# Sums of a Strassen-like product turned into additions, partly made by accumulating DMA transfers, and splits moved between turns

## The chip, the cores and the metric

The kernel runs on one core of one Trainium2 chip. The time is the device time of one execution in microseconds (us). Five engines run side by side with their own instruction streams and meet through semaphores: TensorE (matmuls, named PE in the rows, its weight loads PEld), VectorE (DVE), ScalarE (ACT), GpSimd (POOL) and SyncE (SP). SP, ScalarE and GpSimd also issue DMA transfers (SPq, ACTq, POOLq); 16 DMA engines carry them out.

## The reference

One encoder layer for x of 1024 rows by 2048 columns, all float32:

```
h      = rmsnorm(x) * norm_w
proj   = h @ w_in                     # 2048 -> 4*1024 (attention) + 2*512 + 3*1024 (mLSTM) + 16 gates
attn   = dilated window attention, 8 heads of 128, 3 patterns mixed, q and k normed and rotated
attn  *= silu(z_a)
hm     = mLSTM forward + mLSTM backward, 4 heads (qk 128, v 256), rmsnorm per head
hm     = sigmoid(o_m) * hm * silu(z_m)
x_out  = x + concat(attn, hm) @ w_out # 2048 -> 2048
```

## The kernel before, in words

**Products.** Both projections are one list of 80 groups (GROUPS, line 48). A group makes two output tiles of 128 columns for all 1024 rows, with half of the inner dimension (kh 0 or 1, that is 1024 of 2048). From the third group on it does so by Winograd's form of Strassen's scheme: seven products of a 128x512 weight sum and a 512x512 sum of x's (or y's) blocks, in place of eight. Each float32 operand is split into a rounded part (hi) and the rest (lo), so a product is 12 matmuls of 512 columns: hi*hi, hi*lo, lo*hi for four pieces of 128 (lines 816 to 820). One product is a turn, u, from 14 to 559; g, n = divmod(u, 7). All engines walk the same list of turns in program order, and each has in every turn its share written out: that order and the semaphores are the whole schedule.

**A turn on VectorE** (from line 1895): softmax steps of an attention head; the eviction of product u-1 out of PSUM into xt, for n = 1, 3, 4, 5, 6 (evict, line 1343; ScalarE evicts n = 0 and 2); w_lo of turn u+2 (weight_lo, line 1337); gates; split work; mLSTM or attention steps; sums of y; and one of four weight sums (s_one to s_four) for n = 2, 3, 4, 6. Products alternate between two PSUM banks, so TensorE's turn u+1 waits for the eviction of product u-1. ScalarE makes w_hi of turn u+2 in turn u, after product u-1.

**x's and y's operands.** STAGE (line 54) names the groups at which the right operands are exchanged: group 16 (second half of x, b = 1), 48 (first half again, b = 2), 64 (first half of y, the mLSTM's, b = 3), 72 (second half, the attention's, b = 4). BUILD_AT (line 64) is the turn at which the last group before it starts: 105, 329, 441, 497; an offset counts from there. Operand n may be overwritten once product n of that last group is done, and is read at offset 7 + n. The seven operands are four blocks of x (n = 0, 2, 5's and 6's sources) and the sums T1 to T4 (n = 4, 1, 3, 5), each 512x512, on the chip as 128 partitions by 2048. ScalarE rounds one (t_high, 1083), VectorE takes the rest (t_low, 1442): one such pair is a split. For b = 2 the four sums' splits (KEPT = 1, 3, 4, 5) are loaded from t_dram, where b = 0 left them (t_loads, 514). For b = 3, 4 the operand comes from DRAM into t_lo, ScalarE rounds it into t_hi (y_operands, 1239), VectorE subtracts (y_low, 1829); Y_SPLIT (66) gives the offset of each.

**y's sums** (SUMS = 3, 1, 5, 4, in ty_dram). For the mLSTM's half SP loads three blocks of y of 1 MB at turn 321 (YM_AT) into the arena, VectorE makes three sums over whole blocks, SP stores them; a fourth follows from turn 339 on (ym_loads 657, ym_sums 1801). For the attention's half ya_sums (1816) runs in each head's offset 22: heads 0 to 3 one sum of the head's two halves, stored by SP at 23; heads 4 to 7 three sums with what head h-4 left, which SP loads at 21 and, but for head 7, stores at 23.

**Attention.** Head h starts at turn 357 + 17 h (A_START), so offset 22 of one head is offset 5 of the next. At 4 and 5 VectorE rotates 32 rows of q and of k (rotate, 1698); GpSimd stores them to rot_dram and loads them back in another order (turned_rows, 1953); SP loads the norms, broadcast to all partitions, at 5 and 6 (line 626); VectorE's norm of q and k at 8 and 9 (normed, 1716) reads both and TensorE's scores from 10 on (988) wait for it. SP loads v at 8, z at 9 over ystage, the head's output of before.

**Queues.** SP's queue carries the weights (next_weights, 460), stores of xt, the rows for each mLSTM step (549), loads for heads, and t_dram. GpSimd's carries accumulating stores of xt (added, 1931) and the rotary rows. mLSTM head j starts at turn 112 + 49 j; its y is stored at its offset 61 (m_out). Groups 41 to 47 have no accumulating store.

## Time and profile before

| | us |
|---|---|
| median of 3 runs | 1996.13 (1993.84 to 2001.1) |
| the profiled execution | 1991.36 |
| its span, first to last instruction | 1989.6 |
| TensorE busy | 1947.4 |
| VectorE busy | 1384.3 |
| ScalarE busy | 889.3 |
| GpSimd busy | 222.0 |

The page is one execution. A matmul's end is modelled, and successive matmuls overlap in it, so TensorE's turns are best measured from start to start of their first matmul. The rows of a timeline give start, duration, engine, line, and in brackets the idle time before it and what ended it. The windows give the busy time of each engine in a stretch, the granted clock of TensorE (1.00 is full), the share of the DMA engines' time and what they moved. Groups by form give the count, the busy time and the mean of one.

### The profile page before, as it was taken

To read this page: it belongs to the slowest core of one execution; us is meant where nothing else is said; L and a number is where in the kernel's file an instruction comes from. 1 tells how busy PE (TensorE), PEld (TensorE's weight loads), DVE (VectorE), ACT (ScalarE), POOL (GpSimd) and SP (SyncE) were. 2 spreads that over 40 slices of the span, in tenths; PEclk is the share of its full clock that TensorE was granted. 3 is DMA by queue.
4 is the path that set the end of the run, shared out by engine and by line. 5 is a ranking of instruction groups with operands and counts; after the bars stand their busy time and mean duration, and the time that the engine had idled before them with its cause. 6 is when DMAs were issued, how large, how long until landed. Compare 5 with 4: busy or idle time off the path is not lost.

```text
span 1989.6 us, 27114 instructions
## 1 busy us (share of the span) xinstructions
PE 1947.4 (98%) x9089; PEld 1589.4 (80%) x9089; DVE 1384.3 (70%) x2791; ACT 889.3 (45%) x1422; POOL 222.0 (11%) x240
## 2 busy tenths in 40 slices
PE   8999999999999999999999999999999899999999
PEld 6888887888888888888887878787787677777787
DVE  7677868678768768767767575665666857667655
ACT  6554335344335435334453335545446463455222
POOL 0241000110110010010000111110110111111111
PEclk9999999999999999999999999999999899999999
DMA  6676543564564465365369864462655836347554
GB/s 210 218 272 229 190 160 113 139 151 126 134 162 119 108 159 148 107 159 148 115 206 369 208 154 92 116 175 50 169 121 131 263 75 191 99 119 209 104 117 106
DMA packets 159337, 310.37 MB, mean 156 GB/s; under 512 B 17072, under 2 KB 36048, under 8 KB 155488
## 3 DMA queue, kind: packets, MB, share of 16 engines
q1 hardware_dynamic: 128432, 247.81, 37.8%
q0 software_dynamic: 28608, 53.49, 17.3%
q10 hardware_dynamic: 2160, 7.34, 1.0%
q8 instruction: 74, 1.21, 0.3%
q14 instruction: 63, 0.52, 0.1%
HBM read 198.60 MB, written 118.37 MB: 159 GB/s over the span
## 4 chain that ended last, share of the span: by engine, by line
PE 84%; DMA 5%; DVE 5%; issue 4%; ACT 1%; SPq 0%; POOL 0%; DVEq 0%; ACTq 0%; POOLq 0%
PE ps L816 22%; PE ps L820 21%; PE ps L818 21%; PE ps L1019 3%; PE ps L988 2%; PE ps L1005 2%; DMA arena<-rot_dram 1%; PE ps L957 1%; PE ps L913 1%; PE ps L922 1%; PE ps L916 1%; PE ps L1023 1%; DMA rot_dram<-arena 1%; ACT w_hi L1056 1%; PE ps L1021 1%
## 5 line engine op out<-in xcount | busy, mean ns | idle before, releaser
L816 PE MATMUL ps<-t_hi,w_hi 128*128 128x512 f32 x2184 | 872.0, 399 | 24.4 <-issue 9.7
L820 PE MATMUL ps<-t_hi,w_lo 128*128 128x512 f32 x2184 | 853.5, 391 | 0.0
L818 PE MATMUL ps<-t_lo,w_hi 128*128 128x512 f32 x2184 | 853.2, 391 | 0.0
L816 PEld LDWEIGHTS ps<-t_hi,w_hi 128*128 128x128 f32 x2184 | 411.5, 188 | 125.3 <-issue 45.9
L820 PEld LDWEIGHTS ps<-t_hi,w_lo 128*128 128x128 f32 x2184 | 411.2, 188 | 87.7
L818 PEld LDWEIGHTS ps<-t_lo,w_hi 128*128 128x128 f32 x2184 | 412.1, 189 | 79.6
L1340 DVE TENSOR_TENSOR w_lo<-s_tmp,w_hi 128x512 fp32r<-128x512 f32 x312 | 221.5, 710 | 180.0 <-ACT w_hi L1056 169.2
L1056 ACT CAST w_hi<-s_tmp 128x512 fp32r<-128x512 f32 x312 | 193.9, 622 | 292.7 <-PE ps L820 273.2
L1340 DVE TENSOR_TENSOR w_lo<-w_raw,w_hi 128x512 fp32r<-128x512 f32 x234 | 165.4, 707 | 146.9 <-ACT w_hi L1056 140.6
L1056 ACT CAST w_hi<-w_raw 128x512 fp32r<-128x512 f32 x234 | 145.4, 621 | 225.4 <-PE ps L820 225.3
L413 POOL DMA_DIRECT2D fin_dram<-xt x32 | 28.1, 878 | 850.8 <-ACT xt L1069 829.7
L1064 ACT COPY xt<-ps 128x512 f32<-128x512 f32 x78 | 45.8, 587 | 110.5 <-PE ps L820 110.4
L1200 ACT ACTIVATE arena<-arena,sums 128x704 f32<-128x704 f32 x64 | 56.4, 882 | 79.0 <-DVE sums L1744 79.0
L1069 ACT COPY xt<-ps 128x512 f32<-128x512 f32 x78 | 45.6, 585 | 98.6 <-PE ps L820 98.3
L1370 DVE TENSOR_TENSOR xt<-ps,xt 128x512 f32<-128x512 f32 x78 | 53.8, 689 | 47.4 <-PE ps L820 46.7
L1156 ACT ACTIVATE arena<-arena,g_cols 128x128 f32<-128x128 f32 x64 | 25.9, 405 | 132.1 <-DVE arena L1601 132.1
L1194 ACT ACTIVATE arena<-arena,mins 128x704 f32<-128x704 f32 x64 | 56.7, 887 | 49.1 <-DVE mins L1738 49.0
L1354 DVE TENSOR_TENSOR xt<-ps,xt 128x512 f32<-128x512 f32 x78 | 53.6, 688 | 26.2 <-PE ps L820 25.6
L1373 DVE TENSOR_TENSOR xt<-ps,xt 128x512 f32<-128x512 f32 x78 | 53.7, 688 | 23.6 <-PE ps L820 23.5
L988 PE MATMUL ps<-arena 128*128 128x512 f32 x128 | 65.9, 596 | 3.4 <-DVE arena L1721 2.2
L1364 DVE TENSOR_TENSOR xt<-ps,xt 128x512 f32<-128x512 f32 x78 | 53.6, 688 | 17.2 <-PE ps L820 16.6
L1750 DVE COPY arena<-ps 128x256 f32<-128x256 f32 x64 | 27.0, 422 | 51.9 <-PE ps L1023 33.1
(225 smaller groups left out, 2390.5 us busy)
## 6 DMA issues: line engine op xcount, KB each, us to landing
w_raw<-w_all_dram SPq DMA_DIRECT2D x320, 256.0 KB, 4.0
fin_dram<-xt SPq DMA_DIRECT2D x128, 256.0 KB, 4.3
fin_dram<-xt POOLq DMA_DIRECT2D x128, 256.0 KB, 5.0
arena<-fin_dram SPq DMA_DIRECT2D x64, 512.0 KB, 7.3
outT_dram<-xt POOLq DMA_DIRECT2D x60, 256.0 KB, 4.1
arena<-xT_dram SPq DMA_DIRECT2D x44, 256.0 KB, 6.0
arena<-xT_dram SPq DMA_DIRECT2D x16, 512.0 KB, 4.4
outT_dram<-xT_dram SPq DMA_DIRECT2D x16, 512.0 KB, 5.4
```

The costliest lines, as they stand in the source:

```text
L816: nc.tensor.matmul(ps[:, bank, :], hi, t_hi[:, n, k, :], start=new and k == 0, stop=False, skip_group_check=True)
L818: nc.tensor.matmul(ps[:, bank, :], hi, t_lo[:, n, k, :], start=False, stop=False, skip_group_check=True)
L820: mm = nc.tensor.matmul(ps[:, bank, :], lo, t_hi[:, n, k, :], start=False, stop=k == KP - 1, skip_group_check=True)
L988: nc.tensor.matmul(ps[:, 4, :], q, by_class(a_k)[:, :, h * P:(h + 1) * P], start=True, stop=True)
L1019: nc.tensor.matmul(out, vtok[:, 4 * h + b, :], pT[:, b, :], start=b == 0, stop=False)
L1056: nc.scalar.copy(w_hi[:, b % 3, :], src).then_inc(hi_done, 1)
L1194: nc.scalar.activation(prob[:, i % 2, 0:KEYS], prob[:, i % 2, 0:KEYS], ACT.Exp, bias=mins[:, i % 2:i % 2 + 1], scale=-1.0, accum_out=sums[ ...
L1200: nc.scalar.activation(prob[:, i % 2, 0:KEYS], prob[:, i % 2, 0:KEYS], ACT.Copy, scale=sums[:, 2 + i % 2:3 + i % 2]).then_inc(a_p, 1)
L1340: nc.vector.tensor_tensor(w_lo[:, b % 3, :], src, w_hi[:, b % 3, :].bitcast(F32), ALU.subtract).then_inc(lo_done, 1)
L1354: nc.vector.tensor_tensor(x2, bank, x1, ALU.add).then_inc(ev_d, 1)
L1370: nc.vector.tensor_tensor(x1, bank, x1, ALU.add).then_inc(ev_d, 1)
L1373: nc.vector.tensor_tensor(x2, bank, x2, ALU.add).then_inc(ev_d, 1)
```

## The change

- Signs: T1 to T4, three evictions' results and the weight sums s_one and s_four are negated where needed, so that all sums over blocks of x and y are additions. Evictions n = 1 and 3 become -(bank) - x1 by scalar_tensor_tensor.
- y's sums of the mLSTM half: from turn 226 SP copies blocks of y within DRAM into ty_dram, and GpSimd adds other blocks to them by accumulating transfers, in six steps (YM_STEPS) that wait for one another. ym_loads, ym_sums and their arena tiles go, and so do waits of SP for them.
- y's sums of the attention half: heads 0 to 3 store their upper half for T3 and their one sum three times, at offset 22; heads 4 to 6 have no sum on VectorE, GpSimd adds the halves to three and then one of the sums in DRAM; head 7 adds on VectorE as before.
- Splits: one table of offsets for ScalarE and one for VectorE, for b = 1, 2 and for b = 3, 4. T4's four sums move from offsets 4 and 5 to 6, 7, 8, 9.

```diff
-Y_SPLIT = {3: {3: 0, 5: 1, 6: 2, 8: 3, 9: 4, 10: 5, 11: 6}, 4: {3: 0, 5: 1, 6: 2, 7: 3, 8: 4, 9: 5, 10: 6}}
+HIGH_AT = {1: {1: 0, 2: 1, 4: 2, 6: 3, 7: 4, 9: 6, 10: 5}, 2: {1: 0, 4: 2, 8: 6}}
+LOW_AT = {1: {1: 0, 3: 1, 5: 2, 7: 3, 8: 4, 10: 6, 11: 5}, 2: {1: 0, 5: 2, 8: 6}}
+Y_HIGH = {3: {3: 0, 4: 1, 5: 2, 7: 3, 8: 4, 9: 5, 10: 6}, 4: {3: 0, 5: 1, 6: 2, 7: 3, 8: 4, 9: 5, 10: 6}}
+Y_LOW = {3: {3: 0, 5: 1, 6: 2, 8: 3, 9: 4, 10: 5, 11: 6}, 4: {3: 0, 5: 1, 6: 2, 7: 3, 8: 4, 9: 5, 10: 6}}
 FILL_AT = 45
-YM_AT = 321
...
+YM_STEPS = (226, 231, 236, 322, 328, 333)
...
                 eng.wait_ge(m_out, 16 * M_HEADS)
-                eng.wait_ge(ym_out, 16 * len(SUMS))
+                eng.wait_ge(ym_added, 64)
             else:
-                eng.wait_ge(ya_out if n in SUMS else a_out, 16 * (KP if n in (0, 4) else ATT_HEADS - 1))
+                heads = KP if n in (0, 4) else ATT_HEADS - 1
+                if n == 4:
+                    eng.wait_ge(ya_out, 32 * KP)
+                elif n in SUMS:
+                    eng.wait_ge(ya_added, 32 * (heads - KP))
+                else:
+                    eng.wait_ge(a_out, 16 * heads)
...
                         sp.wait_ge(a_pv, 4 * h)
-                        sp.wait_ge(ya_out, 16 * h)
+                        sp.wait_ge(ya_out, 32 * min(h, KP))
...
                     if h > 0:
                         sp.wait_ge(a_out, 16 * h)
-                        sp.wait_ge(ya_out, 16 * h)
+                        sp.wait_ge(ya_out, 32 * min(h, KP))
+                    if h > KP:
+                        sp.wait_ge(ya_added, 32 * (h - KP))
...
-                if at == 21 and h >= KP:
+                if at == 21 and h == ATT_HEADS - 1:
                     sp.wait_ge(a_pv, 4 * h + 4)
-                    sp.wait_ge(a_out, 16 * (h - KP + 1))
-                    sp.wait_ge(ya_out, 16 * (h - KP + 1))
-                    sp.dma_start(y_sums[:, 0, :], y_dram[ATT_HEADS + h - KP][:, HALF:]).then_inc(ya_in, 16)
-                    sp.dma_start(y_sums[:, 1, :], ty_dram[1, SUMS.index(4)][:, h - KP, :]).then_inc(ya_in, 16)
+                    sp.wait_ge(ya_out, 32 * KP)
+                    sp.dma_start(y_sums[:, 0:2, :], ty_dram[1, 0:2, :, KP - 1, :].rearrange("i p s -> p i s")
+                                 ).then_inc(ya_in, 16)
                 if at == 22 and h < ATT_HEADS - 1:
                     sp.wait_ge(a_y, 4 * h + 4)
                     sp.dma_start(y_dram[ATT_HEADS + h], ystage).then_inc(a_out, 16)
-                if at == 23 and h < ATT_HEADS - 1:
-                    sp.wait_ge(ya_sum, sums_of_y(h + 1))
-                    if h < KP:
-                        sp.dma_start(ty_dram[1, SUMS.index(4)][:, h, :], y_sums[:, 0, :]).then_inc(ya_out, 16)
-                    else:
-                        sp.dma_start(ty_dram[1, 0:3, :, h - KP, :].rearrange("i p s -> p i s"), y_sums
-                                     ).then_inc(ya_out, 16)
-
-            def ym_loads(off):
+                if at == 22 and h < KP:
+                    sp.dma_start(ty_dram[1, SUMS.index(3), :, h, :], ystage[:, HALF:]).then_inc(ya_out, 16)
+                    sp.wait_ge(ya_sum, h + 1)
+                    sp.dma_start(ty_dram[1, 1:4, :, h, :].rearrange("i p s -> p i s"),
+                                 y_sums[:, 0, :].unsqueeze(1).to_broadcast([P, 3, HALF])).then_inc(ya_out, 16)
+
+            def ym_copies(u):
                 y = y_dram[0:ATT_HEADS].rearrange("k p s -> p k s")
-                if off == 0:
-                    sp.wait_ge(m_out, 16 * M_HEADS)
-                    sp.wait_ge(m_g, 2 * M_HEADS)
-                    sp.wait_ge(m_rms, M_HEADS)
-                    sp.wait_ge(m_upd, 16 * M_HEADS)
-                    sp.wait_ge(m_c, 16 * M_HEADS)
-                    sp.wait_ge(m_ops, 16 * M_HEADS)
-                    sp.dma_start(ym_a, y[:, 0:KP, 0:HALF]).then_inc(ym_in, 16)
-                    sp.dma_start(ym_b, y[:, 0:KP, HALF:]).then_inc(ym_in, 16)
-                    sp.dma_start(ym_c, y[:, KP:, HALF:]).then_inc(ym_in, 16)
-                if off in (5, 6, 7):
-                    n, at = ((4, ym_a), (3, ym_b), (1, ym_c))[off - 5]
-                    sp.wait_ge(ym_sum, off - 4)
-                    sp.dma_start(ty_dram[0, SUMS.index(n)], at).then_inc(ym_out, 16)
-                if off == 18:
-                    sp.wait_ge(ym_out, 48)
-                    sp.dma_start(ym_b, y[:, KP:, 0:HALF]).then_inc(ym_in, 16)
-                if off == 22:
-                    sp.wait_ge(ym_sum, 4)
-                    sp.dma_start(ty_dram[0, SUMS.index(5)], ym_b).then_inc(ym_out, 16)
+                if u == YM_STEPS[0]:
+                    sp.wait_ge(m_out, 16 * 2)
+                    for n in (4, 3):
+                        sp.dma_start(ty_dram[0, SUMS.index(n)], y[:, 0:KP, HALF:]).then_inc(ym_out, 16)
+                if u == YM_STEPS[2]:
+                    sp.wait_ge(ym_added, 16)
+                    sp.dma_start(ty_dram[0, SUMS.index(1)], ty_dram[0, SUMS.index(4)]).then_inc(ym_out, 16)
+                if u == YM_STEPS[4]:
+                    sp.wait_ge(ym_added, 48)
+                    sp.dma_start(ty_dram[0, SUMS.index(5)], ty_dram[0, SUMS.index(1)]).then_inc(ym_out, 16)
...
-                    nc.vector.tensor_tensor(x2, bank, x1, ALU.add).then_inc(ev_d, 1)
+                    nc.vector.scalar_tensor_tensor(x2, bank, -1.0, x1, ALU.mult, ALU.subtract).then_inc(ev_d, 1)
...
-                if off in (4, 5):
-                    t_four(1, 2 * off - 8)
-                    t_four(1, 2 * off - 7)
+                if off in (6, 7, 8, 9):
+                    t_four(1, off - 6)
...
             def ya_sums(h):
                 low, high = ystage[:, 0:HALF], ystage[:, HALF:]
+                if KP <= h < ATT_HEADS - 1:
+                    return
                 dve.wait_ge(a_y, 4 * h + 4)
                 if h < KP:
                     dve.wait_ge(a_pv, 4 * h + 4)
-                    nc.vector.tensor_tensor(y_sums[:, 0, :], high, low, ALU.subtract).then_inc(ya_sum, 1)
+                    nc.vector.tensor_tensor(y_sums[:, 0, :], high, low, ALU.add).then_inc(ya_sum, 1)
                     return
-                dve.wait_ge(ya_in, 32 * (h - KP + 1))
-                nc.vector.tensor_tensor(y_sums[:, 1, :], high, y_sums[:, 1, :], ALU.subtract).then_inc(ya_sum, 1)
-                nc.vector.tensor_tensor(y_sums[:, 0, :], high, y_sums[:, 0, :], ALU.subtract).then_inc(ya_sum, 1)
+                dve.wait_ge(ya_in, 16)
+                nc.vector.tensor_tensor(y_sums[:, 1, :], high, y_sums[:, 1, :], ALU.add).then_inc(ya_sum, 1)
+                nc.vector.tensor_tensor(y_sums[:, 0, :], high, y_sums[:, 0, :], ALU.add).then_inc(ya_sum, 1)
                 dve.wait_ge(ya_sum, sums_of_y(h) + 1)
-                nc.vector.tensor_tensor(y_sums[:, 2, :], low, y_sums[:, 1, :], ALU.subtract).then_inc(ya_sum, 1)
+                nc.vector.tensor_tensor(y_sums[:, 2, :], low, y_sums[:, 1, :], ALU.add).then_inc(ya_sum, 1)
 
             def y_low(b, off):
-                n = Y_SPLIT[b].get(off)
...
+            def add_ym(u):
+                y = y_dram[0:ATT_HEADS].rearrange("k p s -> p k s")
+                if u == YM_STEPS[1]:
+                    pool.wait_ge(m_out, 16 * 2)
+                    pool.wait_ge(ym_out, 32)
+                    pool.dma_start(ty_dram[0, SUMS.index(4)], y[:, 0:KP, 0:HALF], accum_op=ALU.add).then_inc(ym_added, 16)
+                if u == YM_STEPS[3]:
+                    pool.wait_ge(m_out, 16 * M_HEADS)
+                    pool.wait_ge(ym_out, 48)
+                    for n in (1, 3):
+                        pool.dma_start(ty_dram[0, SUMS.index(n)], y[:, KP:, HALF:], accum_op=ALU.add).then_inc(ym_added, 16)
+                if u == YM_STEPS[5]:
+                    pool.wait_ge(ym_out, 64)
+                    pool.dma_start(ty_dram[0, SUMS.index(5)], y[:, KP:, 0:HALF], accum_op=ALU.add).then_inc(ym_added, 16)
+
+            def add_ya(h, at):
+                if KP <= h < ATT_HEADS - 1:
+                    if at == 22:
+                        pool.wait_ge(a_y, 4 * h + 4)
+                        pool.wait_ge(ya_out, 32 * KP)
+                        pool.dma_start(ty_dram[1, 0:3, :, h - KP, :].rearrange("i p s -> p i s"),
+                                       ystage[:, HALF:].unsqueeze(1).to_broadcast([P, 3, HALF]), accum_op=ALU.add
+                                       ).then_inc(ya_added, 16)
+                    if at == 24:
+                        pool.wait_ge(ya_added, 32 * (h - KP) + 16)
+                        pool.dma_start(ty_dram[1, SUMS.index(5), :, h - KP, :], ystage[:, 0:HALF], accum_op=ALU.add
+                                       ).then_inc(ya_added, 16)
```

## Rows read from the trace of the kernel before

**Rows 1.** page, part 1 (busy us of each engine) and part 4 (chain of waits by engine).

```profile
PE 1947.4 (98%) x9089; PEld 1589.4 (80%) x9089; DVE 1384.3 (70%) x2791; ACT 889.3 (45%) x1422; POOL 222.0 (11%) x240
...
PE 84%; DMA 5%; DVE 5%; issue 4%; ACT 1%; SPq 0%; POOL 0%; DVEq 0%; ACTq 0%; POOLq 0%
```

**Rows 2.** TensorE timeline (start, duration): turns 106, 119, 326, 329, 343, 357, 425, 442, 459.

```profile
323.86 0.39 PE L816 MATMUL ps<-t_hi,w_hi 128*128 128x512 f32 x1
...
366.31 0.39 PE L816 MATMUL ps<-t_hi,w_hi 128*128 128x512 f32 x1
...
1047.39 0.39 PE L816 MATMUL ps<-t_hi,w_hi 128*128 128x512 f32 x1
...
1058.46 0.47 PE L816 MATMUL ps<-t_hi,w_hi 128*128 128x512 f32 x1 [0.42 <-DVE xt L1370]
...
1100.16 0.39 PE L816 MATMUL ps<-t_hi,w_hi 128*128 128x512 f32 x1
...
1138.24 0.39 PE L816 MATMUL ps<-t_hi,w_hi 128*128 128x512 f32 x1
...
1451.46 0.50 PE L816 MATMUL ps<-t_hi,w_hi 128*128 128x512 f32 x1
...
1531.79 0.50 PE L816 MATMUL ps<-t_hi,w_hi 128*128 128x512 f32 x1
...
1624.78 0.50 PE L816 MATMUL ps<-t_hi,w_hi 128*128 128x512 f32 x1
```

**Rows 3.** windows in head 5: span, busy of PE, PEld, DVE, ACT, POOL, clock, DMA, GB/s.

```profile
1565.00:1567.50 2.50, 0.00 (x0) 0.00 (x0) 2.46 (x4) 0.52 (x1) 1.22 (x3) 0.94 1.06 294
1567.50:1570.00 2.50, 0.55 (x1) 0.50 (x2) 2.50 (x5) 1.22 (x2) 0.87 (x1) 0.50 1.06 403
1570.00:1572.50 2.50, 2.50 (x7) 1.98 (x6) 1.80 (x2) 1.21 (x1) 0.75 (x2) 0.50 1.09 298
```

**Rows 4.** groups by form on VectorE: count, busy us, mean ns, idle before.

```profile
L1354 DVE TENSOR_TENSOR xt<-ps,xt 128x512 f32<-128x512 f32 x78 | 53.6, 688 | 26.2 <-PE ps L820 25.6
...
L1450 DVE TENSOR_TENSOR t_lo<-arena,t_hi 128x2048 fp32r<-128x2048 f32 x14 | 32.1, 2290 | 5.6 <-ACT t_hi L1104 5.5
...
L1861 DVE SCALAR_TENSOR_TENSOR arena<-arena,ncol 128x512 f32<-128x512 f32 x12 | 8.2, 749 | 0.0
...
L1807 DVE TENSOR_TENSOR arena<-arena 128x2048 f32<-128x2048 f32 x1 | 2.3, 2285 | 0.0
```

**Rows 5.** DMA: queues (packets, MB, share of 16 engines), then issues (KB, us to landing).

```profile
q1 hardware_dynamic: 128432, 247.81, 37.8%
q0 software_dynamic: 28608, 53.49, 17.3%
...
outT_dram<-xT_dram SPq DMA_DIRECT2D x16, 512.0 KB, 5.4
...
t_lo<-t_dram SPq DMA_DIRECT2D x4, 1024.0 KB, 9.8
```

**Rows 6.** windows while the kept splits are loaded, columns as before; first and last of six.

```profile
1065.00:1070.00 5.00, 4.41 (x20) 3.38 (x19) 4.26 (x6) 2.92 (x3) 0.00 (x0) 1.00 1.00 363
...
1090.00:1095.00 5.00, 4.00 (x18) 3.02 (x18) 3.47 (x6) 1.24 (x2) 0.37 (x1) 1.00 1.03 345
```

**Rows 7.** timeline of SP's queue, VectorE, GpSimd in heads 1, 5 and 6: start, duration.

```profile
1235.35 0.38 SPq L626 DMA_DIRECT2D arena<-rs_dram  x1
...
1239.77 0.32 SPq L652 DMA_DIRECT2D ty_dram<-arena  x1
...
1246.79 2.05 DVE L1721 SCALAR_TENSOR_TENSOR arena<-arena,spare 128x1024 f32<-128x1024 f32 x1
...
1562.30 0.68 DVE L1824 TENSOR_TENSOR arena<-arena 128x512 f32<-128x512 f32 x1
...
1562.90 0.69 DVE L1825 TENSOR_TENSOR arena<-arena 128x512 f32<-128x512 f32 x1
...
1663.23 0.55 POOL L1962 DMA_DIRECT2D arena<-rot_dram  x1 [4.23 <-DMA rot_dram<-arena]
```

54 lines of the change are left out of this document (20 added, 34 removed).

## The prediction, made before the changed kernel was run

> **What bounds the kernel now.** I read the page's engine totals first: TensorE is busy 98% of 1989.6 us, VectorE 70%, and 84% of the chain of waits is TensorE [rows 1]. So a cheaper VectorE pays only where TensorE stands still or is late. Next I took TensorE's own rows and asked how long one weight product (a turn: 12 matmuls) lasts. Undisturbed, 14 turns take 1138.24 - 1100.16 = 38.08 us, 2.72 us a turn [rows 2]. Stretches against that pace:
> - the splits of x's second half (turns 106 to 118): 366.31 - 323.86 = 42.45 us for 13 turns, 35.4 at the pace: 7.1 us late;
> - the four sums of the mLSTM's y (turns 326 to 328): 1058.46 - 1047.39 = 11.07 us for 3 turns: 2.9 late;
> - the splits of x's first half (329 to 342): 1100.16 - 1058.46 = 41.7 us for 14: 3.6 late;
> - head 5 of the attention, beside which y's first splits lie: 1624.78 - 1531.79 = 92.99 us, and head 4 before it 80.33 us: 12.7 late [rows 2].
> All else that the change touches lies where TensorE keeps its pace, apart from about 1 us a head while the rotary rows come. What fills the four stretches is VectorE: a split costs it 2.29 us, a sum over one of y's blocks 2.29, a sum over one head's half 0.69, or 0.61 where they follow each other [rows 4, 7]. It must take a product out of PSUM (0.69) before TensorE may use that bank again two turns later.
> The granted clock is the second cost. While TensorE stood still in head 5 (0.00 us busy of 2.5), it went from 1.00 over 0.94 to 0.50, that is from 2.4 to 1.2 GHz, and stayed there for 5 us [rows 3]; exposed, that loses 2.5 us.
>
> **The change part by part**, on the profiled execution's own time, 1991.36 us (1.8 of it outside the span). It stands 4.8 us under the median of the runs, 1996.13; differences are added to the median.
>
> *Splits of x's second half: -0.5.* The sums T4 (4 of 0.61) and seven splits (2.2 from start to start) are all still there, 17.8 us, but end at offset 11 instead of 9. I walked VectorE turn by turn: an eviction 0.61, w_lo 0.61, an s sum 0.61. Before, offsets 4 and 5 hold two T4 sums and a split each (5.3 and 4.6 us in a turn of 2.72), so TensorE waits for evictions. After, no turn has over 4.0 (offset 7: eviction, w_lo, one T4, one split). VectorE falls behind by about 1 us in each of offsets 7, 8, 10 and 11. The waits come at product 3 of group 16 (1.2 us) and at product 5, whose split is made one turn before it is read (3.3 us). Its end comes out 1.7 us earlier than now. But the 3.3 us wait stands at the end of the stretch, where VectorE no longer hides a lower clock; at the 5 us of half clock of [rows 3] that gives back up to 2.5. Bounds -1.7 and +0.8; I take the middle.
>
> *y's sums of the mLSTM half leave VectorE: -2.9.* Three of the four whole-block sums (2.29 each, [rows 4]) lie in turns 326 to 328 and are the only extra work there; without them evictions are on time, so the 2.9 goes. The fourth (turn 342) costs TensorE nothing now.
>
> *What replaces them.* Per 1 MB the hardware queue's packets take 37.8% x 1989.6 / 247.8 = 3.0 us of all 16 DMA engines, the software queue's, nearly all of them accumulating, 17.3% x 1989.6 / 53.5 = 6.4 us [rows 5]. The change has four copies of 1 MB within DRAM and four accumulations of 1 MB, for 8 MB of loads and stores: 38 us of DMA for 24. A copy within DRAM of 512 KB lands in 5.4 us now [rows 5]. At turns 226 to 236 TensorE keeps its pace, and each new wait has some 5 turns (14 us) for one transfer. Behind the two copies in SP's queue stand k and q of mLSTM head 2, read four turns on; behind SP's wait at turn 236 the rows of an mLSTM step, behind that at turn 328 the weights of group 48, read four turns on; behind GpSimd's only its stores. I take +0.3 (0 to 3). At turns 322 to 333 VectorE's stores go, but the last accumulation (6.4 us of DMA) becomes ready just when eight 1 MB loads of kept splits run. There the DMA engines are full (1.00 and 1.03 at 363 and 345 GB/s, first and last of six such windows [rows 6]), and the t_lo load takes 9.8 us in the median [rows 5]. Wholly in their way it makes products 339 to 341 6.4 us late, with nothing to hide it; ready before them, 0. I take +2.0. The split of block 2 is made by VectorE a turn after ScalarE's half instead of waiting for it: -0.6 of the 3.6, or nothing.
> Here the Trainium skill, "DMA: Bandwidth & Descriptors", section "Issuing engines are not separate DMA queues", speaks against the change: transfers of all issuing engines end on the same 16 DMA engines and interleave, so moving work to GpSimd's queue makes no bandwidth. By that rule the whole 6.4 counts and the sum is 4.4 us higher; the windows at 1.00 say the engines are full, not whose transfer waits.
>
> *Head 4's three sums (3 x 0.61) leave VectorE, and ScalarE's y splits go a turn earlier: -2.5.* They lie in the very turn that makes product 449 late: the first start at 1562.30 and 1562.90 [rows 7]. Walked again, the eviction comes 1.8 us earlier, and the half that ScalarE makes earlier saves VectorE waits of 0.7. The half clock still costs what VectorE waits for TensorE, 1.1. Bounds -1.0 (more DMA at the same place: 0.75 MB accumulating is 4.8 us) and -5.0 (clock stays up).
>
> *Heads 0 to 3: +1.0.* SP now waits for VectorE's sum one turn earlier, before it loads the first broadcast row: in head 1 that load is issued at 1235.35, the store behind the sum at 1239.77 [rows 7]. So it comes 4.9 us later, behind 0.75 MB of stores (2.3 us). Landing some 7.7 us after issue (a median 5.4 to 5.7 for such a size, and the stores), it comes at 1247.9, and its reader starts at 1246.79 now [rows 7]: so about 1 us of that shows on VectorE. But the second norm, which TensorE waits for, hangs on GpSimd's rotary rows. And v's load at offset 8, with z behind it, waits until 1 MB of stores has landed instead of 0.25. A quarter us in each of four heads; bounds 0 and 3 a head.
>
> *Heads 5 and 6: -0.5.* VectorE gets to the rotary rows 1.8 us earlier, but their store (in head 6 the load behind it goes out at 1663.23 after 4.23 us of waiting [rows 7]) now stands behind a 0.75 MB accumulation in GpSimd's queue, 4.8 us of DMA. The 0.75 MB store on SP goes for it. Bounds -1.8 and +3.0 a head. GpSimd's next wait, for that accumulation, holds only a store back; SP's wait at offset 9 holds z, read four turns later.
>
> *Evictions 1 and 3 become scalar_tensor_tensor: +0.4.* No row has this form on 512 PSUM columns. The same form from SBUF costs 749 ns, a tensor_tensor on the same shape 680 to 690: +0.06 [rows 4, 7]. 156 of them make 9 us, under TensorE except for some seven in the two late stretches. Lower bound 0. The skill's "Vector Engine (DVE) Microarchitecture Reference", section "Points that are easy to get wrong", says that this form halves its rate with two sources in SBUF that are not bf16. The 749 ns row has two fp32 sources in SBUF and shows no halving; by the rule, stretched to PSUM, an eviction would take 1.38 us and seven exposed ones make the sum 4.4 higher.
> The signs themselves cost nothing: add for subtract, same shape.
>
> Sum: -0.5 - 2.9 + 0.3 + 2.0 - 0.6 - 2.5 + 1.0 - 0.5 + 0.4 = -3.3 us, so 1996.1 - 3.3 = 1992.8 us. Own range, from the bounds that pull most: 1986 to 2002.
>
> **The rivals.**
> *The stretches empty (faster).* VectorE is the only cause of all four, and once its peaks are under a turn's length its delay never adds up and the clock never falls. Of 12.7 us in head 5 then 8 go, of 7.1 four, of 3.6 one and a half, with 2.9, less the 1 of heads 0 to 3: 1981 us. For it: the rows show VectorE full there (7.1 to 12.7 us on 1.8 us too much). Against it: seven splits are 15.4 us whatever their order, more than the room in 9 turns.
> *The accumulations become the bound (slower).* One mechanism: transfers that add take 6.4 us of DMA per MB and stand before what TensorE waits for, in the kept splits (up to 6.4 late, and 2.5 of clock) and before the rotary rows of heads 5 to 7 (4.8 each, less 1.8 from VectorE: 9 in all). With 6 us of gains left: +12, 2008 us. It decides once an accumulation delays the rows behind it by more than 3 us. For it: DMA 1.00 in those windows, waits for rotary rows of 4.23 now. Against: all queues together take 37.8 + 17.3% of the DMA engines' time and hardly more [rows 5].
> *The change does not do what it says.* The last split is read one turn after it is made, and the wait only moves: no more than -3 from y's sums, minus what DMA takes: 1996 us, inside no change.
>
> **How the numbers follow.** A measurement of this kernel tells about 0.5%, 10 us, from no change. The forecast at 1992.8 has 0.50, the moved wait 0.09, emptied stretches 0.24, accumulations 0.17. Faster by over 10 us needs 1986: most of the second case, 0.22, and 0.03 from the forecast's low end; slower needs 2006: 0.15. Same: 0.60. The range reaches from just above the emptied stretches' figure to just short of the bound accumulations': 1981 to 2006.
>
> **What would show it.** Turns 326 to 328 at 2.72 us each; product 117 the latest of x's stretch, with 3 us of idle; product 449 less than 3 us late and head 5 in about 90 us; the wait of products 339 to 341 on the t_lo load grown by about 2 us; evictions 1 and 3 at about 0.75 us; heads 1 to 4 at 80 to 81 us. Wrong it is if head 5 falls under 86 us, if the kept splits come over 5 us late, or if a wait for k and q opens at turn 230.

## The result: 1.1% slower

| | median | lowest to highest | runs |
|---|---|---|---|
| before | 1996.99 us | 1993.84 to 2001.1 | 4 |
| after | 2020.22 us | 2017.34 to 2021.07 | 4 |

The ratio is 1.0113, 95% interval 1.0091 to 1.0134. The forecast, 1992.8 us, and its range (to 2006) both missed; the price of the rival that named accumulating transfers as a bound, 2008, was too low too.

The profile after: first the page's busy times, chain and queues (to be set beside [rows 1, 5]) and VectorE's group of an eviction in the new form (beside [rows 4]); then DMA issues with KB each and the median us to landing, that is from the issue of a transfer to the event that reports it complete:

```profile
PE 1952.5 (97%) x9089; PEld 1595.5 (79%) x9089; DVE 1370.4 (68%) x2778; ACT 887.7 (44%) x1422; POOL 232.3 (12%) x250
...
q1 hardware_dynamic: 126384, 242.83, 36.5%
q0 software_dynamic: 32352, 60.83, 19.5%
...
PE 83%; DMA 6%; issue 5%; DVE 4%; ACT 1%; POOL 1%; SPq 0%; DVEq 0%; ACTq 0%; POOLq 0%
...
L1352 DVE SCALAR_TENSOR_TENSOR xt<-ps,xt 128x512 f32<-128x512 f32 x78 | 53.6, 687 | 25.2 <-PE ps L818 24.7
```

```profile
t_lo<-t_dram SPq DMA_DIRECT2D x4, 1024.0 KB, 15.9
...
ty_dram<-y_dram POOLq DMA_DIRECT2D x4, 1024.0 KB, 15.7
...
ty_dram<-arena POOLq DMA_DIRECT2D x3, 768.0 KB, 11.0
```

VectorE has 14 us less to do and the kernel is 23 us slower. TensorE has the same 9089 matmuls. DMA has gone from 5 to 6% of the chain and "issue" from 4 to 5%: 1% is 20 us. A kept split's t_lo now lands after 15.9 us in place of 9.8 [rows 5].

The starts of the turns that [rows 2] show before the change (all but 357 and 425), and between them those of three products that waited long, 117, 341 and 452 (TensorE's timeline: start, duration, in brackets the idle time before and what ended it):

```profile
323.92 0.39 PE L814 MATMUL ps<-t_hi,w_hi 128*128 128x512 f32 x1
...
358.94 0.47 PE L814 MATMUL ps<-t_hi,w_hi 128*128 128x512 f32 x1 [2.94 <-DVE t_lo L1448]
...
366.09 0.39 PE L814 MATMUL ps<-t_hi,w_hi 128*128 128x512 f32 x1
...
1048.23 0.39 PE L814 MATMUL ps<-t_hi,w_hi 128*128 128x512 f32 x1
...
1056.39 0.39 PE L814 MATMUL ps<-t_hi,w_hi 128*128 128x512 f32 x1
...
1098.28 0.76 PE L814 MATMUL ps<-t_hi,w_hi 128*128 128x512 f32 x1 [5.85 <-DMA t_lo<-t_dram]
...
1106.40 0.39 PE L814 MATMUL ps<-t_hi,w_hi 128*128 128x512 f32 x1
...
1557.06 0.50 PE L814 MATMUL ps<-t_hi,w_hi 128*128 128x512 f32 x1
...
1607.80 0.77 PE L814 MATMUL ps<-t_hi,w_hi 128*128 128x512 f32 x1 [6.50 <-DVE t_lo L1818]
...
1652.14 0.50 PE L814 MATMUL ps<-t_hi,w_hi 128*128 128x512 f32 x1
```

From such starts every stretch has its length. Here and in the table of the experiments it is the time in us from the start of the stretch's first product to the start of the first product behind it:

| turns | what lies there | before | after | |
|---|---|---|---|---|
| 106-118 | splits of x's second half | 42.45 | 42.17 | -0.3 |
| 222-244 | first steps of the mLSTM half's sums | 75.82 | 76.51 | +0.7 |
| 320-328 | VectorE's whole-block sums, before | 27.39 | 24.48 | -2.9 |
| 329-342 | kept splits | 41.70 | 50.01 | +8.3 |
| 374-441 | attention heads 1 to 4 | 321.63 | 340.78 | +19.2 |
| 442-458 | head 5 | 92.99 | 95.08 | +2.1 |
| 459-496 | head 6 and most of head 7 | 183.92 | 183.92 | 0.0 |
| 497-510 | y's second splits | 44.07 | 45.55 | +1.5 |
| all others | | | | +0.2 |

The sum is +28.8 us, between two profiled executions of which before's was 5.6 us under its median of 1996.99. Some of that is chance: in several traces of kernels with the same code there, one turn of 2.7 us (449, 502, 509) takes 4.4 or 5.3.

The two large losses are both waits for DMA, at places where TensorE kept its pace or nearly so. Windows (columns as in [rows 3]) of the changed kernel, beside the first two accumulations and at product 341's wait:

```profile
1040.00:1045.00 5.00, 5.00 (x24) 4.14 (x23) 2.62 (x4) 3.06 (x6) 0.00 (x0) 1.00 1.08 235
...
1095.00:1100.00 5.00, 1.72 (x4) 1.46 (x5) 0.71 (x2) 0.00 (x0) 0.86 (x1) 0.69 0.87 288
1100.00:1105.00 5.00, 5.00 (x15) 3.92 (x15) 1.14 (x2) 0.62 (x1) 0.24 (x1) 0.62 0.00 1
```

With accumulations in flight the DMA engines are full (1.08) at 235 GB/s; with plain loads they were full at 363 [rows 6]. And TensorE's wait in the kept splits costs twice: the clock falls, so turn 341 lasts 5.26 us where 2.72 would do.

In head 2, SP's queue, GpSimd's queue, VectorE and TensorE of the changed kernel (start, duration):

```profile
1324.98 0.34 SPq L658 DMA_DIRECT2D y_dram<-arena  x1
...
1325.38 0.42 SPq L660 DMA_DIRECT2D ty_dram<-arena  x1
...
1329.38 0.37 SPq L662 DMA_DIRECT2D ty_dram<-arena  x1
...
1329.85 1.10 SPq L635 DMA_DIRECT2D arena<-rs_dram  x2
...
1331.40 0.57 POOL L1968 DMA_DIRECT2D rot_dram<-arena  x1 [2.95 <-DVE arena L1711]
...
1340.03 0.55 POOL L1973 DMA_DIRECT2D arena<-rot_dram  x1 [7.49 <-DMA rot_dram<-arena]
...
1340.68 2.06 DVE L1718 SCALAR_TENSOR_TENSOR arena<-arena,spare 128x1024 f32<-128x1024 f32 x1 [3.73 <-DMA arena<-rot_dram]
...
1347.60 2.08 PE L986 MATMUL ps<-arena 128*128 128x512 f32 x2 [4.00 <-DVE arena L1718]
```

SP waits 4 us for VectorE's sum (between the first two stores and the third), then both broadcast rows (0.5 MB each) go out together behind 0.75 MB of stores, and 1.5 us later GpSimd's second rotary store (128 KB) joins them. It lands 7.5 us after GpSimd began to wait. VectorE waits for the rows, TensorE's scores wait 4.00 us for VectorE, and in 1345 to 1350 the granted clock is 0.61. That it is the rotary rows, and not the broadcast ones that the prediction walked, follows from the landings: the broadcast rows landed at 1337.8 and 1339.3, q's rotary rows at 1340.7, where VectorE's norm of q starts, and k's at 1345.5, where its norm of k starts.

### The profile page after: what moved, and what is told of

Its sections match the earlier page's. It is cut to its first block, busy times and chain, and to the rows that moved or that the text cites. A ratio compares the mean times of both kernels' runs of the same rounds, so it can differ in the third digit from the quotient of the medians.

```text
span 2018.4 us, 27095 instructions
## 1 busy us (share of the span) xinstructions
PE 1952.5 (97%) x9089; PEld 1595.5 (79%) x9089; DVE 1370.4 (68%) x2778; ACT 887.7 (44%) x1422; POOL 232.3 (12%) x250
## 4 chain that ended last, share of the span: by engine, by line
PE 83%; DMA 6%; issue 5%; DVE 4%; ACT 1%; POOL 1%; SPq 0%; DVEq 0%; ACTq 0%; POOLq 0%
PE ps L814 21%; PE ps L818 21%; PE ps L816 21%; DMA arena<-rot_dram 3%; PE ps L1017 2%; PE ps L986 2%; PE ps L1003 1%; PE ps L955 1%; PE ps L911 1%; PE ps L920 1%; DMA rot_dram<-arena 1%; PE ps L914 1%; DMA t_lo<-t_dram 1%; PE ps L1021 1%; PE ps L900 1%
## 5 line engine op out<-in xcount | busy, mean ns | idle before, releaser
L1368 DVE TENSOR_TENSOR xt<-ps,xt 128x512 f32<-128x512 f32 x78 | 53.7, 689 | 55.3 <-PE ps L818 54.6
L1352 DVE SCALAR_TENSOR_TENSOR xt<-ps,xt 128x512 f32<-128x512 f32 x78 | 53.6, 687 | 25.2 <-PE ps L818 24.7
L1371 DVE TENSOR_TENSOR xt<-ps,xt 128x512 f32<-128x512 f32 x78 | 53.6, 687 | 25.0 <-PE ps L818 24.9
L1362 DVE TENSOR_TENSOR xt<-ps,xt 128x512 f32<-128x512 f32 x78 | 53.6, 687 | 18.6 <-PE ps L818 18.0
```

The costliest lines, as they stand in the source:

```text
L1352: nc.vector.scalar_tensor_tensor(x2, bank, -1.0, x1, ALU.mult, ALU.subtract).then_inc(ev_d, 1)
L1362: nc.vector.tensor_tensor(x3, bank, x3, ALU.add).then_inc(ev_d, 1)
L1368: nc.vector.tensor_tensor(x1, bank, x1, ALU.add).then_inc(ev_d, 1)
L1371: nc.vector.tensor_tensor(x2, bank, x2, ALU.add).then_inc(ev_d, 1)
```

## The experiments

All are the changed kernel with the edit shown. Stretches are in us; "heads 1-4" is turns 374 to 441.

| kernel | median | ratio to before (95%) | 106-118 | 329-342 | 357-373 | heads 1-4 | head 5 | 459-496 |
|---|---|---|---|---|---|---|---|---|
| before | 1997 | 1 | 42.45 | 41.70 | 71.92 | 321.63 | 92.99 | 183.92 |
| after | 2020.22 | 1.0113 (1.0091-1.0134) | 42.17 | 50.01 | 71.80 | 340.78 | 95.08 | 183.92 |
| e1_order | 2009.06 | 1.0065 (1.0047-1.0083) | 40.59 | 49.34 | 72.23 | 328.12 | 95.74 | 184.34 |
| e2_bytes | 2012.3 | 1.0080 (1.0058-1.0103) | 42.16 | 49.79 | 71.91 | 333.03 | 96.24 | 183.21 |
| e3_ym_late | 2022.13 | 1.0129 (1.0111-1.0147) | 42.19 | 41.06 | 80.63 | 339.98 | 96.29 | 183.52 |
| e4_ym_last | 2012.76 | 1.0082 (1.0052-1.0111) | 40.55 | 44.10 | 71.63 | 338.52 | 95.87 | 185.03 |
| e5_add_late | 2012.16 | 1.0075 (1.0053-1.0097) | 42.16 | 48.28 | 70.72 | 340.97 | 90.15 | 179.69 |
| e6_x_order | 2016.54 | 1.0099 (1.0071-1.0126) | 39.03 | 50.37 | 72.25 | 339.50 | 95.95 | 182.86 |
| e7_calm | 1994.31 | 0.9991 (0.9975-1.0008) | 42.19 | 49.88 | 73.56 | 322.44 | 91.46 | 179.35 |
| e8_att_undone | 2003.4 | 1.0033 (1.0017-1.0048) | 42.18 | 49.03 | 70.18 | 322.50 | 92.38 | 183.41 |
| e9_rows_sp | 2028.06 | 1.0150 (1.0120-1.0180) | 42.19 | 49.52 | 71.78 | 339.93 | 105.17 | 185.03 |
| e10_plain | 2019.63 | 1.0108 (1.0081-1.0135) | 42.18 | 46.91 | 71.27 | 341.18 | 95.89 | 183.75 |
| b1_best | 1980.57 | 0.9923 (0.9897-0.9949) | 39.03 | 41.55 | 70.47 | 321.91 | 91.09 | 179.01 |
| b2_best | 1986.94 | 0.9948 (0.9928-0.9967) | 38.99 | 41.80 | 73.82 | 324.12 | 92.37 | 179.65 |

Each ratio is against runs of the kernel before on the same chip (its median was 1997.19, 1993.89 and 1996.16 us in the three groups of experiments). The stretches are read from one execution each, and the same code varies: turns 106 to 118 from 40.55 to 42.19 us in the ten traces with the changed kernel's code there, 329 to 342 from 48.27 to 50.37 in eight, 357 to 373 from 70.19 to 73.56 in nine, heads 1 to 4 from 338.52 to 341.18 in seven. A difference of that size is not a reading. In the expectations a long turn is sometimes named by its own number where the wait is at the start of the next product (turn 451: product 452; turn 358: product 359).

**Heads 1 to 4: order or bytes.** e1_order:

```diff
-                if at == 22 and h < KP:
+                if at == 23 and h < KP:
                     sp.dma_start(ty_dram[1, SUMS.index(3), :, h, :], ...)
```

> The changed kernel with one thing moved back: in heads 0 to 3 SP issues T3's store, the wait for VectorE's sum and the three-way store at offset 23, behind the first broadcast row, as before the change; the bytes stay. Theory A (order): heads 1 to 4 lost 19.2 us because the wait and the stores stand ahead of the broadcast rows and the rotary rows. Then most comes back: heads 1 to 4 at 81 to 82 us each, the kernel at about 2004 us (2000 to 2008). Rival B (bytes): it is the 0.75 MB more of stores beside the rotary rows, whatever their place: heads 1 to 4 stay at 84 to 87 us and the kernel at 2016 to 2020.

e2_bytes:

```diff
-                    sp.dma_start(ty_dram[1, SUMS.index(3), :, h, :], ystage[:, HALF:]).then_inc(ya_out, 16)
                     sp.wait_ge(ya_sum, h + 1)
-                    sp.dma_start(ty_dram[1, 1:4, :, h, :]..., y_sums[:, 0, :]...to_broadcast([P, 3, HALF]))
+                    sp.dma_start(ty_dram[1, SUMS.index(4), :, h, :], y_sums[:, 0, :]).then_inc(ya_out, 16)
```

> The changed kernel with the order kept (the wait for the sum and the store ahead of the broadcast rows, at offset 22) but only T4's 0.25 MB stored there; T3's store and two of the three-way store's copies are left out in heads 0 to 3, so those parts of y's sums are not the reference's (their places are filled at turns 250, 260 and 270, where TensorE keeps its pace). Rival B (bytes): heads 1 to 4 fall back by 12 to 19 us, the kernel to 2001 to 2008. Theory A (order): the wait alone costs; heads 1 to 4 keep most of +19.2, the kernel stays over 2012. If both this and the other kernel recover most, it is the product of the two: the loads wait behind what is stored ahead of them, and either a short store or a late one does no harm.

Measured: the order alone (e2_bytes) costs 333.03 - 321.63 = 11.4 us, the bytes alone (e1_order) 6.5, the two together 19.2. So neither theory is the whole: e1_order missed theory A's 2004 us by 5 and its range by 1, e2_bytes, at 2012.3, sits at the edge of its 2012, and the parts nearly add (17.9 of 19.2).

**The same bytes at another time.** e7_calm stores T4's 0.25 MB at offset 23 and makes the other three sums' first terms by copies within DRAM at offset 30; the accumulations of heads 4 to 6 stand two turns later:

```diff
+                if at == 30 and h < KP:
+                    sp.dma_start(ty_dram[1, SUMS.index(3), :, h, :], y_dram[ATT_HEADS + h][:, HALF:])
+                    sp.dma_start(ty_dram[1, 1:3, :, h, :]..., ty_dram[1, SUMS.index(4), :, h, :]...)
...
-                    if at == 22:
+                    if at == 24:
                         pool.wait_ge(a_y, 4 * h + 4)
...
-                    if at == 24:
+                    if at == 26:
                         pool.wait_ge(ya_added, 32 * (h - KP) + 16)
```

> The changed kernel with both remedies for the attention half: in heads 0 to 3 only T4's 0.25 MB is stored, at offset 23, and the other three sums get their first term by copies within DRAM at offset 30, where no row that TensorE waits for is on its way; the accumulating transfers of heads 4 to 6 stand at 24 and 26. Theory: the 19.2 us of heads 1 to 4 come back but for 0 to 3 (80.5 to 81.5 us each), head 5 and 6 stay at 90 and 79 us: the kernel at 1994 to 1997 us. Rival: the bytes cost wherever they stand, as the accumulations of turns 343 to 351 did; then heads 1 to 4 keep 2 us or more each and the kernel is over 2000.

Measured: 1994.31 us, ratio to before 0.9991 (0.9975 to 1.0008), heads 1 to 4 at 322.44. The same amount reaches DRAM as in the changed kernel, with 0.75 MB a head more read, and it costs 0.8 us in four heads, which is within chance. Its head 2, to be set beside the fence above:

```profile
1324.86 0.37 SPq L635 DMA_DIRECT2D arena<-rs_dram  x1
...
1329.24 0.43 SPq L635 DMA_DIRECT2D arena<-rs_dram  x1
...
1331.40 0.58 POOL L1978 DMA_DIRECT2D arena<-rot_dram  x1
...
1335.61 0.55 POOL L1978 DMA_DIRECT2D arena<-rot_dram  x1 [3.63 <-DMA rot_dram<-arena]
...
1343.39 1.13 PE L991 MATMUL ps<-arena 128*128 128x512 f32 x2 [0.35 <-DVE arena L1723]
```

The first broadcast row is 4.4 us ahead of the second again, the second rotary store is waited for 3.63 us in place of 7.49, TensorE 0.35 in place of 4.00.

e8_att_undone takes the attention half's sums back to VectorE and to the stores of before, with additions:

```diff
-                    add_ya(h, u - A_START[h])
...
-                if KP <= h < ATT_HEADS - 1:
-                    return
...
+                nc.vector.tensor_tensor(y_sums[:, 1, :], high, y_sums[:, 1, :], ALU.add).then_inc(ya_sum, 1)
```

> The changed kernel with the attention half's sums as before the change (VectorE's three sums in heads 4 to 7, 0.25 MB stored by SP at offset 23 in heads 0 to 3), with additions for subtractions; the mLSTM half's sums in DRAM, the splits' tables and the evictions by scalar_tensor_tensor stay. Theory: what is left of the change costs +8.3 in the kept splits, -2.9 at turns 326 to 328, -0.3 in x's second half, +1 elsewhere, and the earlier y splits of ScalarE give 0 to 1 back in head 5: 2003 us (2001 to 2005), so the attention part is some 17 to 20 us of the 24. Rival: the evictions' new form and the tables cost in the heads too; then heads 1 to 4 stay over 81.5 us each and the kernel over 2007.

Measured: 2003.4 us, 17 less than the changed kernel; heads 1 to 4 at 322.50. The new eviction form and the tables cost the heads nothing that shows. The time from product 448's start to 449's tells what the two edits of head 5 did: 7.56 us before, 5.76 in the changed kernel, 7.56 here, where ScalarE's earlier table is kept and the three sums are back. All of the 1.8 us is the sums'.

**The kept splits.** e3_ym_late and e4_ym_last:

```diff
-YM_STEPS = (226, 231, 236, 322, 328, 333)
+YM_STEPS = (226, 231, 236, 343, 347, 351)
```

```diff
-YM_STEPS = (226, 231, 236, 322, 328, 333)
+YM_STEPS = (226, 231, 236, 322, 328, 343)
```

> The changed kernel with the last three steps of the mLSTM half's sums at turns 343, 347 and 351 in place of 322, 328 and 333, behind the loads of the kept splits. Theory A: the accumulating transfers hold up those loads; turns 329 to 342 fall from 50.0 us to 41 to 42 and products 339 to 341 start on time as before, and turns 343 to 356 keep 38.1 us, since nothing is read from DRAM in a hurry there: the kernel comes 8 us lower, 2012 (2010 to 2014). Rival: the loss there is of the splits' new table (block 2's split, late VectorE) or of the loads themselves; the stretch stays at 48 to 50 us and the kernel at 2020. Second rival: the transfers only move their harm, and turns 343 to 373 get 3 us or more.

> The changed kernel with only the last accumulating transfer of the mLSTM half's sums moved, from turn 333 to 343; the two of turn 322 and the copy of turn 328 stay. Theory A: the kept splits' loads are held up by the one transfer that is issued among them (turn 333, landing 17 us later): turns 329 to 342 fall from 50.0 to 41 to 43 us, and since it has landed by turn 350, no store of head 0's tiles stands behind it in GpSimd's queue, and product 358 keeps its 6.4 us (it had 14.4 when all three steps stood at 343 to 351): the kernel at 2011 to 2013 us. Rival: the two of turn 322, and the copy for which SP waits at 328, push the loads late; then the stretch stays at 47 us or more.

Measured: e3_ym_late has 9.0 us less in the kept splits (41.06) and 8.8 more in head 0: the second rival. Its windows while head 0's q and k are loaded, ScalarE's wait for weights and product 359:

```profile
1130.00:1135.00 5.00, 5.00 (x24) 4.14 (x23) 2.93 (x5) 1.24 (x2) 0.94 (x2) 1.00 1.10 247
1135.00:1140.00 5.00, 5.00 (x24) 4.14 (x23) 1.70 (x3) 0.00 (x0) 1.64 (x2) 1.00 1.10 262
1140.00:1145.00 5.00, 2.06 (x10) 1.36 (x8) 0.00 (x0) 0.00 (x0) 0.00 (x0) 1.00 1.09 299
```

```profile
1145.41 0.62 ACT L1054 CAST w_hi<-w_raw 128x512 fp32r<-128x512 f32 x1 [10.80 <-DMA w_raw<-w_all_dram]
...
1153.62 0.50 PE L814 MATMUL ps<-t_hi,w_hi 128*128 128x512 f32 x1
```

The DMA engines are full at 247 to 299 GB/s. A transfer of weights (256 KB) takes 18.1 us to land, where the median is some 4; ScalarE waits 10.80 us for it and comes late to the squares of q and k too. So 14.44 us lie between products 358 and 359, where 6.41 did. e4_ym_last: the one transfer issued among the loads is 5.9 of the 8.3 us, and at turn 343 it harms nothing (71.63 in head 0). In b1_best, with the same steps, the stretch is at 41.55, so the other 2.4 of e4_ym_last's is no fixed cost of the first two accumulations: with the same code in this stretch the two traces differ by 2.5 us, and the one transfer's share is anything from 5.9 to 8.5.

e10_plain makes that transfer a plain copy; it leaves out the addition for the sum n = 5.

```diff
-                    pool.dma_start(ty_dram[0, SUMS.index(5)], y[:, KP:, 0:HALF], accum_op=ALU.add)
+                    pool.dma_start(ty_dram[0, SUMS.index(5)], y[:, KP:, 0:HALF])
```

> The changed kernel with the last accumulating transfer of the mLSTM half's sums (turn 333, 1 MB) issued as a plain copy of the same 1 MB from the same queue at the same turn: T3's counterpart for n = 5 then lacks its first term. Theory A: it is the addition in the transfer that costs the DMA engines double; turns 329 to 342 fall from 50.0 to 43 to 46 us, and the DMA engines move over 330 GB/s in each 5 us there. Rival: any 1 MB more beside the eight kept splits' loads costs this; the stretch stays at 48 to 50.5 us.

Measured: 46.91 us, 0.9 over the top of theory A's range, and 1.1 under the rival's. Both have a part: against e4_ym_last and b1_best (44.10 and 41.55) a plain copy of 1 MB there costs 2.8 to 5.4 us, and against the eight traces with the accumulation (48.27 to 50.37) the addition costs 1.4 to 3.5 more. With one trace of the plain copy, closer figures are not to be had. The transfer itself lands after 11.4 us, where the accumulation of the same turn took 17.1. The windows agree: 419 GB/s at a share of 1.01 where the changed kernel, in the same window, had 354 at 1.09.

```profile
1075.00:1080.00 5.00, 5.00 (x24) 4.14 (x23) 3.33 (x6) 0.95 (x2) 0.00 (x0) 1.00 1.01 419
```

The kernel's median is only 0.6 us lower: in the profiled execution turns 497 to 510 (47.80) and head 5 were 3.1 us longer than in the changed kernel's, at code that is the same.

**Head 5: the queue or the engines.** e5_add_late moves the accumulations of heads 4 to 6 from offsets 22 and 24 to 24 and 26, the last two hunks of e7_calm's diff, and nothing else.

> The changed kernel with the accumulating transfers of heads 4 to 6 issued at offsets 24 and 26 in place of 22 and 24, so behind the stores and loads of the rotary rows in GpSimd's queue. Theory A: product 451's wait (6.5 us, rotary rows landing at 1603) comes from the 0.75 MB accumulation that stands ahead of them; head 5 falls from 95.1 us to 88 to 90 and the kernel by 5 to 8, to 2012 to 2015. Rival: the rows are late from all the DMA traffic there (y's first splits are loaded beside them), wherever the accumulation stands: head 5 stays at 93 to 95 and the kernel within 2 us of 2020.

Measured: head 5 at 90.15, heads 6 and 7 at 179.69 (4.2 under the changed kernel), the kernel 8 us lower. GpSimd's wait for the second rotary store, 10.97 us in the changed kernel, is 3.50 (the first fence is the changed kernel's, the second e5_add_late's):

```profile
1603.16 0.58 POOL L1973 DMA_DIRECT2D arena<-rot_dram  x1 [10.97 <-DMA rot_dram<-arena]
```

```profile
1592.36 0.57 POOL L1973 DMA_DIRECT2D arena<-rot_dram  x1 [3.50 <-DMA rot_dram<-arena]
...
1593.52 1.67 POOL L1956 DMA_DIRECT2D ty_dram<-arena  x1
```

That fits a queue served in order as well as full engines. e9_rows_sp leaves the accumulation where it is and lets SP move heads 5 to 7's rotary rows:

```diff
+                if h > KP and at == 5:
+                    for i in range(2):
+                        sp.wait_ge(a_rot, 8 * h + 4 * i + 4)
+                        sp.dma_start(rot_dram[h, i], turn[i][:, 0:256])
+                if h > KP and at == 6:
+                    ...
+                        sp.dma_start(halves((raw_a, raw_b)[i][0:ROT]), rot_dram[h, i]...)
...
             def turned_rows(h, at):
+                if h > KP:
+                    return
```

> The changed kernel, accumulating transfers of heads 4 to 6 at 22 and 24 as it has them, but in heads 5 to 7 SP stores and loads the rotary rows (at offsets 5 and 6, both stores together), so that no accumulation stands ahead of them in their own queue. Theory A (queue): the store that took 13.5 us to land took it because it stood behind the 0.75 MB accumulation in GpSimd's queue; product 451's wait goes and head 5 is at 89 to 91 us. Theory B (bandwidth): the accumulation fills the DMA engines whoever issues the rows; their landing stays at 9 us or more each and head 5 at 93 to 97. SP's own work waits meanwhile; weights late by a turn would show as waits for w_raw.

```profile
1585.40 4.16 SPq L640 DMA_DIRECT2D rot_dram<-arena  x2
...
1598.54 0.33 SPq L645 DMA_DIRECT2D arena<-rot_dram  x1
...
1610.61 2.02 DVE L1731 SCALAR_TENSOR_TENSOR arena<-arena,spare 128x1024 f32<-128x1024 f32 x1 [11.95 <-DMA arena<-rot_dram]
```

```profile
1595.00:1600.00 5.00, 5.00 (x22) 4.10 (x21) 2.41 (x3) 2.53 (x3) 0.86 (x1) 0.92 1.10 287
```

```profile
rot_dram<-arena SPq DMA_DIRECT2D x2, 128.0 KB, 12.4
```

Measured: head 5 at 105.17 us. Head 5's two stores of rows (the last fence is of 1580 to 1605 alone), now in SP's queue, land after 12.4 us in the median, their two loads after 11.1; in the changed kernel GpSimd's second store took 13.2. My theory of the queue fell: the rows are late because the DMA engines are full (shares 1.02 to 1.10 at 287 to 313 GB/s from 1590 to 1605), whoever issues them. The comparison is not a clean one: in SP's queue the rows stand behind y's store and the first broadcast row (0.5 MB each), and GpSimd, no longer held by the rows, issues its accumulation 3 us earlier. But the transfers of the other queues tell the same: beside the accumulation that broadcast row took 11.1 us, weights from SP 11.7 to 14.7 and a 1 MB load from ScalarE's queue 18.4. Beyond the range that I gave, SP waited for the rows and held its later loads up too.

**Order of x's last two splits.** e6_x_order:

```diff
-HIGH_AT = {1: {..., 7: 4, 9: 6, 10: 5}
+HIGH_AT = {1: {..., 7: 4, 9: 5, 10: 6}
-LOW_AT = {1: {..., 8: 4, 10: 6, 11: 5}
+LOW_AT = {1: {..., 8: 4, 10: 5, 11: 6}
-                if off in (6, 7, 8, 9):
-                    t_four(1, off - 6)
+                for kt in {6: (0, 1), 7: (2,), 8: (3,)}.get(off, ()):
+                    t_four(1, kt)
```

> The changed kernel with the last two splits of x's second half in the order in which they are read: block 5 (read by product 117) is split at offset 10 and block 6 (product 118) at 11, and T4's four sums lie at offsets 6, 6, 7, 8 in place of 6, 7, 8, 9. Theory A: product 117's wait (2.9 us) and the half clock behind it come from the split that is made one turn before it is read; turns 106 to 118 fall from 42.2 to 37.5 to 39.5 us, the kernel by 3 to 4 us. Rival: VectorE is simply full there, and the wait moves to products 116 and 118: 41 to 42.5 us, the kernel unchanged within 1 us. All else as in the changed kernel: 2016 to 2020 us.

Measured: 39.03 us, 3.1 less, and 39.03 and 38.99 in both last kernels; traces of the old order have 40.55 to 42.19, so the gain is 1.5 to 3.2. Product 117's wait of 2.94 us is gone. A part of it moves, as the rival had it: product 118 waits 0.77 us, and 115 waits 1.48 in place of 0.90. The kernel's median is 3.7 us under the changed one's, but the two ratios' intervals overlap; the stretch is the evidence.

**All remedies.** b1_best is e7_calm with e4_ym_last's steps and e6_x_order's tables; b2_best is b1_best with

```diff
-YM_STEPS = (226, 231, 236, 322, 328, 343)
+YM_STEPS = (226, 231, 236, 322, 343, 347)
```

> All remedies together: the kernel e7_calm (first terms of heads 0 to 3 by copies at offset 30, accumulations of heads 4 to 6 at 24 and 26), the last accumulation of the mLSTM half at turn 343, and the order of the last two splits of x's second half from e6_x_order. By theory the parts add: 1994.3 - 5.9 (kept splits 44.1 us) - 3.1 (turns 106 to 118 at 39.0) = 1985.3 us (1982 to 1990), 0.4% under the kernel before. Rival: the gains hide in one another or in the lower clock, and it stays at 1990 to 1994.

> As b1_best, with the copy for which SP waits moved too: steps at turns 322, 343, 347. Theory A: what is left in the kept splits (44.1 against 41.7 us before) is SP's wait for the first two accumulations at turn 328, or the accumulations themselves beside the loads; with the copy late the stretch is at 41 to 42, and the last accumulation (turn 347) is done before head 0's loads need the DMA engines: 1983 us (1980 to 1988). Rival: the last accumulation ends beside head 0's q and k, as it did with steps at 343, 347, 351, and product 358 is 2 to 8 us late: 1985 to 1991.

Measured: b1_best 1980.57 us (6 runs, 1979.02 to 1988.21), ratio to before 0.9923 (0.9897 to 0.9949): it is faster than both kernels, by 0.8% and some 2%, and 1.4 us under its own range. b2_best 1986.94 (0.9948, 0.9928 to 0.9967): nothing gained in the kept splits (41.80), and 3.4 us lost in head 0 and 2.3 in head 3. The time is in the rival's range, but its mechanism is not there: the last accumulation had landed at 1115.6, before head 0's q and k were issued (1134), and product 359 comes 6.41 us after 358 as in b1_best. The 3.4 us lie in turns 366 and 367, and e7_calm, with nothing moved there, has 73.56 against b2_best's 73.83. So what costs b2_best its 6 us stays open. TensorE's starts at turns 106, 119, 329, 343, 442, 459 in b1_best:

```profile
323.85 0.39 PE L819 MATMUL ps<-t_hi,w_hi 128*128 128x512 f32 x1
...
362.88 0.39 PE L819 MATMUL ps<-t_hi,w_hi 128*128 128x512 f32 x1
...
1053.09 0.39 PE L819 MATMUL ps<-t_hi,w_hi 128*128 128x512 f32 x1
...
1094.64 0.39 PE L819 MATMUL ps<-t_hi,w_hi 128*128 128x512 f32 x1
...
1525.10 0.50 PE L819 MATMUL ps<-t_hi,w_hi 128*128 128x512 f32 x1
...
1616.19 0.50 PE L819 MATMUL ps<-t_hi,w_hi 128*128 128x512 f32 x1
```

## Why the prediction was wrong, step by step

- *Heads 0 to 3, +1.0 (bounds 0 and 3 a head): measured +19.2, in the turns of heads 1 to 4.* This is the step that failed. The chain was right: the load behind the wait for VectorE's sum, behind 0.75 MB. But I priced the load that I saw delayed, and left aside the second norm, which "hangs on GpSimd's rotary rows", as if those stood apart. They share the DMA engines. Each head lost 2.5 to 6.9 us. In head 2, the one walked here, it went through the rotary rows, and the clock fell behind the wait. Even the upper bound, 12 us in all, was too low: it held neither the clock nor a transfer of another queue.
- *Kept splits, +2.0 (0 to 6.4): measured +8.9 at turns 339 to 341; block 2's split gave 0.5 back at turn 333, -0.6 forecast.* The mechanism and the place were right (products 340 and 341 wait for t_lo), the size not: the waits alone are 1.33 + 5.85 us, and the half clock behind them adds 2.4 at turn 341. My own bound for the second rival had 2.5 for the clock, the forecast did not. The price of 6.4 us for one accumulation wholly in the way was near: moving that one transfer gave 5.9 us (e4_ym_last) and 8.5 (b1_best). It was the +2.0, a guess between 0 and 6.4, that was wrong.
- *Head 5, -2.5: measured +2.1.* Product 449 came 1.8 us earlier as walked, all of it by the three sums; the 0.7 for ScalarE's earlier table is not seen there, and head 5 of e8_att_undone, which keeps it, is 0.6 under before's, within chance. The loss belongs to another term, the -0.5 of heads 5 and 6: product 452 waits 6.50 us for a split that VectorE makes late, as it waited 6.00 for rotary rows. Its bound of +3.0 was under what the 0.75 MB accumulation did; head 6 lost 0.3. I named the wrong cause for it as well: GpSimd's queue, where e9_rows_sp speaks for the engines.
- *y's sums leave VectorE, -2.9: measured -2.9*, with turns 326 to 328 at 2.72 us each.
- *Steps at 226 to 236, +0.3: measured +0.7*, at turn 230, which k and q of mLSTM head 2 reach late; the sign of a wait there that I had asked for. It is +0.4 to +1.4 in twelve of the thirteen traces, and +4.5 in e8_att_undone, with the same code there.
- *Splits of x's second half, -0.5: measured -0.3.* The walk had the waits at the right products (115 comes 1.05 us late against 1.2 forecast, 117 waits 2.94 against 3.3). That the sum agrees so well is partly luck: two of the ten traces with this code have -1.9. The split placed one turn before it is read cost 1.5 to 3.2 us, which e6_x_order recovers.
- *y's second splits (turns 497 to 510): no term, measured +1.5.* Product 502 waits 2.11 us for VectorE, which had waited 1.97 for ScalarE's rounding in front of a split; before, 0.19 and 0.62. The stretch has 45.25 to 50.20 us in the thirteen traces with the change's code there, against 44.06 before. Why ScalarE is later there is not shown.
- *The new eviction form, +0.4: measured 0*, 687 ns against 688 [rows 4]. The halving that the Trainium skill states ("Vector Engine (DVE) Microarchitecture Reference", "Points that are easy to get wrong") is for two sources in SBUF; with one of them in PSUM the row shows none, as the 749 ns row [rows 4] with both in SBUF shows none either.
- The rule that I had weighed against one step, and not followed, held: by the Trainium skill's "DMA: Bandwidth & Descriptors", "Issuing engines are not separate DMA queues", another engine's queue makes no bandwidth. The trace agrees: in e9_rows_sp rows land 12.4 us after issue from SP's queue beside an accumulation from GpSimd's. I never asked what it does to the rotary rows.
- *The rivals.* "The accumulations become the bound" had the sign, the kept splits and head 5. Its 2008 us was 12 too low, since two thirds of the loss (19.2 of 28.8 us net) are not by accumulations: in heads 1 to 4 the stores are plain ones.
